# Prompt attention: the selected part of query tile 4 is given a first unit for its oldest key tile

## What is computed

```python
gk = gather(ks_b.transpose(0, 3, 1, 2, 4), idx_t)
gv = gather(vs_b.transpose(0, 3, 1, 2, 4), idx_t)
...
s2 = jnp.einsum('btgrd,bgtksd->bgtrks', q, gk).astype(jnp.float32) * scale
s2 = s2 + bias_s.transpose(0, 1, 2, 5, 3, 4)
...
p_s = masked_softmax(s2.reshape(B, G, T, R, K * SB), valid.reshape(B, G, T, R, K * SB))
o_sel = jnp.einsum('bgtrks,bgtksd->btgrd', p_s.reshape(s2.shape).astype(gv.dtype), gv)
```

## Time and profile before

| | us |
|---|---|
| median of 3 runs | 1113.71 |
| lowest, highest | 1111.62, 1114.09 |
| the profiled execution | 1115.21 |
| its span, first to last instruction | 1113.2 |

### The profile page before, as it was taken

One profiled execution on the slowest core, in us unless ns is written; L12 is line 12 of the kernel. 1 busy time (PEld: TensorE's weight loads), 2 busy tenths in 40 slices (PEclk: granted clock), 3 DMA queues, 4 the chain that ended last, 5 costly groups with the idle time before them and its releaser, 6 DMA issues. The chain is left out here.

```text
span 1113.2 us, 22587 instructions
## 1 busy us (share of the span) xinstructions
PE 1075.2 (97%) x8368; PEld 763.3 (69%) x8368; DVE 624.6 (56%) x1627; ACT 362.5 (33%) x893; POOL 86.5 (8%) x184
## 2 busy tenths in 40 slices
PE   6899999999999999998999999999999999999997
PEld 3455599998886677776776657664544576777775
DVE  0645323463423477769677766742323588888883
ACT  0322001121112475546555555631112133333330
POOL 0210100110000011101101010011000200000000
PEclk9899999999999999999999999999999999999998
DMA  9933270001006240000000000005794467878781
GB/s 355 310 115 94 72 211 2 16 19 72 1 1 122 44 116 2 1 1 2 1 2 1 2 1 2 1 1 119 169 307 152 142 217 262 271 274 275 261 251 51
DMA packets 96612, 120.25 MB, mean 108 GB/s; under 512 B 31569, under 2 KB 65380, under 8 KB 95480
## 3 DMA queue, kind: packets, MB, share of 16 engines
q1 hardware_dynamic: 96504, 118.81, 34.4%
HBM read 104.41 MB, written 14.36 MB: 107 GB/s over the span
## 5 line engine op out<-in xcount | busy, mean ns | idle before, releaser
L549 PE MATMUL PS<-AR 128*128 128x256 f32 (+2 forms) x896 | 219.7, 403 | 0.0
L549 PEld LDWEIGHTS PS<-AR 128*128 128x128 f32 x896 | 167.8, 190 | 45.2 <-issue 6.2
L2090 PE MATMUL PS<-AR 128*128 128x512 f32 x256 | 112.3, 592 | 0.0
L1747 PE MATMUL PS<-CA,AR 128*128 128x128 f32 x704 | 111.4, 282 | 0.8 <-ACT AR L1821 0.8
L963 DVE TENSOR_TENSOR AR<-PS,AR 128x256 f32<-128x256 f32 (+2 forms) x80 | 36.2, 452 | 134.4 <-PE PS L549 134.3
L1747 PEld LDWEIGHTS PS<-CA,AR 128*128 128x128 f32 x704 | 77.0, 143 | 44.6 <-issue 31.7
L1821 ACT ACTIVATE AR<-PS 128x512 f32<-128x512 f32 (+1 forms) x108 | 58.2, 546 | 125.1 <-PE PS L1747 124.5
L1725 PE MATMUL PS<-AR 128*128 128x65 f32 (+1 forms) x688 | 89.3, 271 | 0.0
L2090 PEld LDWEIGHTS PS<-AR 128*128 128x128 f32 x256 | 47.5, 190 | 54.0 <-issue 54.0
L1725 PEld LDWEIGHTS PS<-AR 128*128 128x128 f32 x688 | 84.3, 192 | 0.0
L1806 ACT ACTIVATE AR<-PS,SM_ 128x512 f32<-128x512 f32 (+4 forms) x192 | 76.6, 471 | 15.9 <-DVE SM_ L1914 8.8
(11 more groups left out here) (364 smaller groups left out, 1622.9 us busy)
## 6 DMA issues: line engine op xcount, KB each, us to landing
AR<-in_cache_nsa SPq DMA_DIRECT2D x128, 256.0 KB, 5.0
AR<-in_cache_mla SPq DMA_DIRECT2D x128, 96.0 KB, 3.7
AR<-in_x_prompt SPq DMA_DIRECT2D x16, 512.0 KB, 4.6
AR<-in_w_ada SPq DMA_DIRECT2D x3, 2048.0 KB, 11.4
AR<-in_w_in SPq DMA_DIRECT2D x6, 1024.0 KB, 8.4
AR<-in_w_ada SPq DMA_DIRECT2D x8, 512.0 KB, 4.3
AR<-in_w_out SPq DMA_DIRECT2D x4, 1024.0 KB, 10.0
AR<-in_w_out SPq DMA_DIRECT2D x2, 2048.0 KB, 17.5
```

The costliest lines, as they stand in the source:

```text
L549: mm = pe.matmul(bank[:, 0:WIDE[g]], tokens[:, k, :], w, start=(fresh and k == 0), stop=(last and k == 3), skip_group_check=True)
L1747: mm = pe.transpose(PS[:, 4 + c % 2, P * (t - t0):P * (t - t0) + P], tile(u, t), ident)
L2090: mm = pe.matmul(PS[0:n, 2 + 2 * (m % 2) + c, :], YTO[m % 2][:, f, 0:n], weights[:, f, 512 * c:512 * c + 512], start=(f == 0), stop=(f == 7))
```

## The change

The condition for the "old" unit becomes a function `apart(kind, i)`, which holds for the local stages from tile 4 and for selected stage 4. So selected stage 4 gets an "old" unit of eight heads on key tile 0 and four units of key tiles 1 to 4, which take one slot each in place of both. For this unit DVE copies the scores without a mask (the copy with `tensor_copy`, now L1855). `TURNS_BACK` now holds for selected stage 4 too, so its values take the crossed form, its exponentials are summed by ACT, and its groups are copied out and turned back. The wait ahead of the keeping, for the last exponentials that read `BTX[:, :, 256:384]`, now names the last earlier unit for which `apart` holds, whatever its stage. Behind it, the five new slot users shift which of the two slots each later local unit takes; what is computed there is the same.

```diff
--- before.py
+++ after.py
@@ -1515,10 +1515,15 @@
         STAGES = [(i, kind) for i in range(4) for kind in ("sel", "win", "cmp", "mla")]
         STAGES += [(i, "cmp") for i in range(4, NT)] + [(i, kind) for i in range(4, NT) for kind in ("win", "sel", "mla")]
         UNITS, GROUPS = [], []
+
+        def apart(kind, i):
+
+            return kind == "win" and i >= 4 or kind == "sel" and i == 4
+
         for i, kind in STAGES:
             k0 = max(0, i - 4) if kind == "win" else 0
             nb = 1 if kind == "cmp" else i + 1 - k0
-            if kind == "win" and i >= 4:
+            if apart(kind, i):
                 UNITS.append(("old", i, 0, [(r, g) for r in range(R) for g in range(G)], k0, 1, len(GROUPS)))
             for half in range(2):
                 if kind == "cmp":
@@ -1542,7 +1547,7 @@
         holds, toggle = [-1, -1], 0
         pholds, turn = [-1] * 4, 0
         for u, (kind, i, half, heads, k0, nb, og) in enumerate(UNITS):
-            if nb > 4 and kind != "win":
+            if nb > 4 and not apart(kind, i):
                 SLOTS.append((0, 1))
             else:
                 SLOTS.append((toggle,))
@@ -1579,7 +1584,7 @@
         NCH = len(CHUNKS)
         EVN = [sum(BY_A[k] == BY_A[c] for k in range(c + 1)) for c in range(NCH)]
         AV_LAG = 2
-        TURNS_BACK = [kind == "sel" and i >= 5 or kind == "win" and i >= 4 for kind, i, half, last in GROUPS]
+        TURNS_BACK = [kind in ("sel", "win") and i >= 4 for kind, i, half, last in GROUPS]
         OUT_AT = {c: [og for og, g in enumerate(GROUPS) if TURNS_BACK[og] and CH_OF[g[3]][-1] + AV_LAG + 1 == c]
                   for c in range(NCH + 4)}
         FIN_AT = {c: [og for og, g in enumerate(GROUPS) if CH_OF[g[3]][-1] + AV_LAG + (2 if TURNS_BACK[og] else 1) == c]
@@ -1696,7 +1701,7 @@
                         mm = pe.matmul(scores(u, gi, o, o + P * n), QRT[rg, half, q], KRT[rg, ks],
                                        start=False, stop=True)
                     else:
-                        keys = KSELT if kind == "sel" else KWINT
+                        keys = KSELT if GROUPS[og][0] == "sel" else KWINT
                         mm = pe.matmul(scores(u, gi, o, o + P * n), QT[64 * g:64 * g + 64, r, q], keys[64 * g:64 * g + 64, ks],
                                        start=True, stop=True)
                 if TWO[u] or m == len(runs) - 1:
@@ -1795,7 +1800,7 @@
                     if room_for(u, gi):
                         act.wait_ge(s_trc, room_for(u, gi))
                     r, g = heads[gi]
-                    sc = BTX[:, R * g + r, 256:384] if kind == "win" and lo else PSF[:, o + lo:o + hi]
+                    sc = BTX[:, R * g + r, 256:384] if apart(kind, i) and lo else PSF[:, o + lo:o + hi]
                     if crossed(u):
                         slot = 2 * (r % 2) + g + (4 if lo else 0)
                         if og >= 4:
@@ -1841,13 +1846,17 @@
             def oldest(u):
                 _, i, half, heads, k0, nb, og = UNITS[u]
                 dve.wait_ge(s_qk, QK0[u + 1])
-                past = [v for v in WHOLE if UNITS[v][0] == "win" and UNITS[v][1] == i - 1] if i > 4 else []
+                past = [v for v in WHOLE if v < u and apart(*UNITS[v][0:2])]
                 if past:
                     dve.wait_ge(s_exp, EXP0[past[-1] + 1])
                 kept = BTX[:, :, 256:384].rearrange("p (g r) c -> p g r c", g=G)
-                dve.tensor_tensor(kept, scores(u, 0, 0, 1024).rearrange("p (g r c) -> p g r c", g=G, c=P),
-                                  wmask.rearrange("p (g r c) -> p g r c", g=1, r=1).to_broadcast([P, G, R, P]), ALU.add)\
-                    .then_inc(s_old, 1)
+                sc = scores(u, 0, 0, 1024).rearrange("p (g r c) -> p g r c", g=G, c=P)
+                if GROUPS[og][0] == "sel":
+                    ins = dve.tensor_copy(kept, sc)
+                else:
+                    ins = dve.tensor_tensor(kept, sc, wmask.rearrange("p (g r c) -> p g r c", g=1, r=1)
+                                            .to_broadcast([P, G, R, P]), ALU.add)
+                ins.then_inc(s_old, 1)
                 dve.wait_ge(s_old, sum(OLD[:u + 1]))
                 oldest_minima(0)
 
@@ -1865,7 +1874,7 @@
                 if NTH[u] >= 2:
                     dve.wait_ge(s_exp, EXP0[WHOLE[NTH[u] - 1]])
                 nm = NM[:, NTH[u] % 2, 0:len(heads)]
-                kept = kind == "win" and i >= 4
+                kept = apart(kind, i)
                 near = {"cmp": 64, "mla": P, "sel": min(256, P * nb), "win": min(256, P * nb)}[kind]
                 far = 0 if kind == "cmp" else P * (nb - kept) - near
                 if far:
```

## The result

The changed kernel takes 1121.55 us (median of 7 runs, 1115.46 to 1122.47), the kernel before in the same measurement 1111.62 (7 runs, 1110.54 to 1114.09). The ratio, which goes by all runs and not by the two medians, is 1.0065 with a 95% interval of 1.0041 to 1.009: slower, as forecast, and more than forecast. Measured again, the same file gave 1117.01 (12 runs, 1114.27 to 1122.71) and a ratio of 1.0035 [1.0014, 1.0056]; over all 19 runs the median is 1117.16 and the mean 1118.4. The profiled execution took 1117.07 us with a span of 1114.9, 1.7 longer than before.

The account below looks back on a forecast made before the run. PE was taken to bound the kernel, with its own work binding the selected stage of tile 4. Work of -1.3 us plus 4.6 us of new waiting made +3.3 on the 1113.7 us median: 1117.0 us, range 1115.0 to 1119.9.

Parts of the forecast that it names:

- PE's own work: Selected stage 4 on PE: crossed values save 3.0 us, oldest tile adds 1.09, turning back 0.64; sum -1.3 us.
- The walk: Step-by-step queue timing from local to selected stage of tile 4: 4.6 us of added waiting, +3.3 in sum; chance 0.43.
- ACT's drain: Drain of the last local unit's first chunk, queued behind the first selected exponentials; from 540.0, 0.60 us long.
- tell-tale (3): Profile sign: PE wait of 2 to 3.3 us at the last local unit's third-chunk turns, one below 1.2 after.
- the third wait: PE waiting for the drain of the first selected unit, after the second selected unit's scores; 0.9 us.
- Rival A: Granted clock falls behind the new 2.8 us PE wait: +0.6 to +2.0, taken 1.4; total +4.7, 1118.4; chance 0.30.
- the buffer's wait: DVE's copy of the oldest tile's scores waits until the last local exponentials stop reading that buffer, 533.4.
- ACT's order: ACT's queue puts the first selected unit's exponentials ahead of the drain of the last local unit's first chunk.
- the long wait: PE idle ahead of the last two turns of the last local unit, until 540.65; 2.8 us.
- B: PE's own work decides and the new waits do not come: -1.3 us, 1112.4; chance 0.08.
- C: Shorter stall, as links put in series overlap: half of it, +1.5 to +2 us, 1115.4; chance 0.11.
- D: Longer stall, if DVE's late finish also hits the next groups: +6 us, 1119.7; chance 0.05.

Follow-up runs that it names:

- Experiment 7: Changed kernel with the kept scores in a buffer of their own and the last local unit's chunk drained ahead of the first selected exponentials; median 1113.89 us, ratio 1.001.
- experiment 4: Kernel before with only the crossed form of the values in selected stage 4, no unit for the oldest tile; median 1113.21 us, ratio 0.9989.
- experiment 3: Changed kernel with three unread 128x512 multiplications on PE, put ahead of the last local unit's third chunk; median 1117.01 us, ratio 1.0022.
- experiment 6: Changed kernel with selected stage 4's kept scores in a buffer of their own, ACT's order unchanged; median 1114.22 us, ratio 1.0009.
- experiment 2: Changed kernel with the last local unit's chunk drained on ACT ahead of the first selected exponentials; median 1112.37 us, ratio 0.9999.
- after: First profile of the changed kernel, no further edit; the profiled execution took 1117.07 us.
- again: Changed kernel measured once more, no edit; median 1117.01 us, ratio 1.0035.
- look: Changed kernel a third time, no edit, one run; 1122.38 us.
- unit only: Changed kernel without the TURNS_BACK line: unit for the oldest tile kept, values in their old form; median 1117.33 us, ratio 1.0039.
- the held kernel before: Kernel before with unread multiplications in PE's waits at the attention's start and in local stage 4 (1.95 us); median 1111.39 us, ratio 0.9976.
- the held changed one: Changed kernel with unread multiplications in three PE waits: attention start, local stage 4, behind the last local unit; median 1115.12 us, ratio 1.0018.

## Why the prediction was right, and where it was off

**PE's own work, -1.3.** Right. Experiment 7 gives it without the stall: the distance less its waits is 35.45 - 0.21 = 35.24 us before and 35.58 - 0.94 - 0.67 = 33.97 there, 1.27 less. One step behind it was attributed wrongly. The text put the whole 0.75 us a unit on the values. From start to start, a unit's values do fall from 2.17 to 1.40, but its turns grow from 1.15 to 1.39 beside them, and its scores fall from 1.28 to 1.06 since the oldest tile leaves it. The form alone, in experiment 4, brings 0.46. The sum held because it used the measured period of a local unit, 3.85, and that came: 549.07 to 552.91.

**The walk.** The copy took 1.23 us as taken, and started at 533.50 where 533.4 was written. First selected exponentials: 538.77 for 538.7. ACT's drain: 540.11 for 540.0. PE's turns: 540.85 for 540.65. The waits that were tell-tale (3) came at the named instructions. The poorest match was the third wait, 0.52 for 0.9. Half clock can hide it, as the text on A said: it is 0.93, 0.52 and nothing in the three traces of the changed kernel, and 0.95 where the clock stayed at 1.00 (experiment 3). The sum of the walk, +3.3, measured +3.57 with the clock held.

**Of the two causes one decides.** The walk named the buffer's wait and ACT's order. Without the first the long wait is 1.0 us shorter and stays (experiment 6); without the second it is gone (experiment 2).

**Rival A.** The size was right: 1.4 with ends of 0.6 and 2.0. Measured are 1.2 and 1.6, and 0.6 in the third trace (39.65 less 39.02). Its chance was not. The text held it less likely than the plain walk (0.30 against 0.43), because the clock had stood at 1.00 through 1.95 us before 521.29. That was one trace's luck: in four others it is at 0.50 from 524.9 to 525.5 on, behind the same wait. The fall came in all four traces in which the long wait is whole (after, again, look, unit only) and even behind 1.81 us. The forecast should have been A's, +4.7 (in the traces +4.8, +5.1 and +4.2). That its 1118.4 is also the mean of all 19 runs is luck: the means lie 7.2 us over the kernel before in the first measurement and 3.7 in the second.

**The total.** The median of the first seven runs, 1121.55, lies 1.65 us over the range's end; their mean, 1119.56, and the median of all 19 runs lie in it. The step that failed is the last one: adding a difference read in one stage to the median, and making the range from that stage's bounds alone. A run of either kernel also carries falls of the clock in places that no edit touches: 3.95 us at the start of the attention in one trace, 4.7 behind it (547.45 less 542.75) in the trace from which the forecast was made. Four of those seven runs have a mean granted clock of 0.980 to 0.987 and lie at 1121.55 to 1122.47; the other three, at 0.991 and 0.992, lie at 1115.46 to 1117.07, inside the range. For a median of few runs that spread belonged in the range.

**Rivals B, C and D** did not occur, and no stage behind gave anything back: from local stage 5 to the end, the held kernel before takes 544.36 us and the held changed one 544.37, each with one stretch of half clock there.

**Open.** It stays open in which executions the clock falls at 388, 525, 893 or 1102 us. The instructions and waits are the same, and no run here was made to tell. Whether the change makes these falls more frequent was not settled either: of 19 runs of it 8 are over 1120 us, of 35 of the kernel before, measured with the second batch, none is (highest 1119.0). But +4.8 shifts that mark to 1115.2, and 9 of the 35 are over it.

## What to carry to other kernels

Before copying a scheme to the next stage, walk the seam where the last unit of the old form and the first of the new one share queues; here the steady rhythm won 1.3 us and the waits at the seams lost 4.8. Ask at a seam for two things: a buffer that the new stage writes while the old one still reads, and a drain queued behind work that needs what the drain lets go on. When a change is worth a few us and single runs of one kernel differ by nine, compare one stage's distance in the traces, read where each trace has half clock before comparing spans, and take more than one trace before saying that a wait leaves the clock alone.

## What the runs showed of the hardware that was not expected

- One instruction stream with one pattern of waits (0.72 us of work, then 1.22 idle, a few small jobs, 0.20 idle) is followed by a granted clock of 1.00 in one execution and of 0.50 for some 10 us in another; the price is 3.95 us.
- Two short fillings in two waits gave the kernel before 0.9976 [0.996, 0.9992] and 12 runs within 3.3 us, with a trace that is no faster where the clock had held anyway. Three other kernels with them spread over 4.8 to 6.8 us, so how far this carries is open.
- One and the same PE wait of 1.95 us in local stage 4 left the clock at 1.00 in six of the ten traces in which it isn't filled, and was followed by 0.50 in four. One of 1.81 us in the changed stage was followed by 0.50 in its one trace, and those of 2.60 to 2.79 us in all four.
- Stretches of half clock behind the attention cost 1.7 us (759.9 to 763.3 in the trace after) and 3.0 us (1094.0 to 1100.9 in the one before): 544.4 and 547.45 us in place of 542.75 from local stage 5 to the end.
